# A two-stack transformer on one core: set-up constants in another queue, another order in the hybrid mixers, and mixer B's probabilities transposed head by head

## What is computed

```python
def hybrid_mixer(h, w_in, ...):
    q, k, v, z, xbc, dt = split(h @ w_in)
    attn = dilated_attention(rotary(q), rotary(k), v)          # 8 heads
    xs, bm, cm = split(silu(causal_depthwise_conv(xbc)))
    dt = softplus(dt + dt_bias)
    m = (cm @ bm.T) * segsum_exp(dt * a_neg)                   # exp(cs[l] - cs[s]) for l >= s, per head, chunks of 128
    y = m @ (xs * dt) + state_part + d_skip * xs
    return concat(attn, rmsnorm(y * silu(z))) @ w_out
# mixer B: 16 heads, compressed-block attention plus a selected-block and a window branch
o = g0 * softmax(q @ kc) @ vc + g1 * softmax(q @ k1) @ v1 + g2 * softmax(q @ k2) @ v2
```

## Time and profile before

| | us |
|---|---|
| median of 3 runs | 2666.72 (2665.9 to 2670.82) |
| the profiled execution, its own time | 2666.94 |
| span from its first to its last instruction | 2664.7 |
| PE busy | 2594.8 (97%) |
| DVE, ACT, POOL busy | 1808.8, 1449.8, 189.1 |
| mean granted TensorE clock | 0.994 of full |

### The profile page before, as it was taken

How to read it: one execution, slowest core, us unless ns; L and a number is a source line. 1 busy time by engine, 2 the same in 40 slices (tenths; PEclk the granted TensorE clock), 3 DMA queues, 4 the chain that set the end, 5 groups by cost and what they waited for, 6 DMA issues and landing times.

```text
span 2664.7 us, 43984 instructions
## 1 busy us (share of the span) xinstructions
PE 2594.8 (97%) x15457; PEld 2259.9 (85%) x15457; DVE 1808.8 (68%) x2578; ACT 1449.8 (54%) x2304; POOL 189.1 (7%) x266
## 2 busy tenths in 40 slices
PE   7999999999999999999989999999999999999999
PEld 7888888888888878888888688888888888888887
DVE  6866668666766676676676666676656667666766
ACT  4655546455555565555555655555556555555654
POOL 2010001000000030000001200000010000002000
PEclk9999999999999999999999999999999999999999
DMA  6559845487566447656654266566446666653664
GB/s 188 160 171 236 226 152 159 143 238 210 170 194 189 137 148 219 190 177 195 190 175 134 88 200 190 178 196 189 151 138 194 189 205 181 199 164 129 184 191 144
DMA packets 587098, 473.78 MB, mean 178 GB/s; under 512 B 19676, under 2 KB 546416, under 8 KB 586480
## 3 DMA queue, kind: packets, MB, share of 16 engines
q1 hardware_dynamic: 582768, 457.37, 56.6%
q0 software_dynamic: 3312, 14.36, 2.4%
q10 hardware_dynamic: 912, 0.63, 0.1%
HBM read 469.09 MB, written 6.37 MB: 178 GB/s over the span
## 4 chain that ended last, share of the span: by engine, by line
PE 86%; DVE 5%; ACT 3%; DMA 2%; issue 2%; POOL 1%; DVEq 1%; SPq 0%; POOLq 0%; ACTq 0%
PE acc L784 20%; PE gu L751 14%; PE tp L751 14%; PE tp L758 7%; PE gu L758 7%; PE acc L817 3%; DVE lo_a L454 2%; ACT hi_a L442 1%; DMA raw_a<-in_w_in 1%; PE acc L1463 1%; PE gu L1421 1%; PE gu L1430 1%; PE acc L1465 1%; PE acc L1464 1%; PE gu L1422 1%
## 5 line engine op out<-in xcount | busy, mean ns | idle before, releaser
L454 DVE TENSOR_TENSOR lo_a<-raw_a,hi_a 128x2048 fp32r<-128x2048 f32 (+1 forms) x313 | 711.1, 2272 | 359.1 <-ACT hi_a L442 357.7
L442 ACT ACTIVATE hi_a<-raw_a 128x2048 fp32r<-128x2048 f32 (+1 forms) x313 | 591.5, 1890 | 125.2 <-PE acc L1465 31.7
L751 PE MATMUL tp<-xT,hi_a 128*128 128x512 f32 x1600 | 398.4, 391 | 0.0
L751 PE MATMUL gu<-xT,hi_a 128*128 128x512 f32 x1600 | 397.9, 391 | 0.0
L751 PEld LDWEIGHTS gu<-xT,hi_a 128*128 128x128 f32 x1600 | 294.0, 188 | 56.9
L751 PEld LDWEIGHTS tp<-xT,hi_a 128*128 128x128 f32 x1600 | 293.4, 188 | 56.4
L784 PE MATMUL acc<-hi_b,h_hi 128*128 128x512 f32 x760 | 298.6, 393 | 1.3 <-issue 1.2
L784 PE MATMUL acc<-lo_b,h_hi 128*128 128x512 f32 x760 | 297.9, 392 | 0.0
L784 PE MATMUL acc<-hi_b,h_lo 128*128 128x512 f32 x760 | 295.7, 389 | 0.0
L466 DVE TENSOR_TENSOR lo_b<-raw_b,hi_b 128x1024 fp32r<-128x1024 f32 x210 | 255.9, 1219 | 0.0
L843 ACT ACTIVATE arena<-arena 128x256 f32<-128x256 f32 x200 | 83.6, 418 | 279.0 <-DVE arena L906 279.0
(11 more groups left out here) (344 smaller groups left out, 4100.8 us busy)
## 6 DMA issues: line engine op xcount, KB each, us to landing
raw_a<-in_ffn_w_in SPq DMA_DIRECT2D x352, 512.0 KB, 5.8
raw_b<-in_ffn_w_out SPq DMA_DIRECT2D x176, 512.0 KB, 3.7
raw_a<-in_w_in SPq DMA_DIRECT2D x52, 512.0 KB, 4.7
raw_a<-in_w_gate SPq DMA_DIRECT2D x44, 512.0 KB, 5.6
raw_a<-in_w_up SPq DMA_DIRECT2D x44, 512.0 KB, 6.8
raw_b<-in_w_down SPq DMA_DIRECT2D x44, 512.0 KB, 4.7
raw_a<-in_w_out SPq DMA_DIRECT2D x24, 512.0 KB, 4.3
raw_a<-in_c_w_in SPq DMA_DIRECT2D x24, 512.0 KB, 4.4
```

What stands on the lines that cost most here:

```text
L442: nc.scalar.activation(a_view(hi_a, par)[:, :, 0:width], a_view(raw_a, par)[:, :, 0:width], ACT.Copy).then_inc(a_hi, 1)
L454: nc.vector.tensor_tensor(a_view(lo_a, par)[:, :, 0:width], a_view(raw_a, par)[:, :, 0:width], a_view(hi_a, par)[:, :, 0:width].bitcast(F3 ...
L751: nc.tensor.matmul(banks[:, e, :], w_hi[:, kt, e * P:(e + 1) * P], xT[:, :, kt, :], start=(kt == 0), stop=False)
```

## The change

Four pieces. (1) **Set-up**: POOL no longer issues the nine `rest_loads`; SyncE issues them, and the seven `late_loads`, behind slot 1 and ahead of slot 2. (2) **The head of the hybrids**: `rows_pe` moves from the end of slot 0 to the middle of slot 1, between its high and low parts, with `columns_pe` behind it in the first hybrid; DVE makes the low part of slot 1 ahead of the diagonal; POOL loads the masks only after `rb_ready`. (3) **Further on in the hybrids**: at p = 11 DVE evacuates the values ahead of the low part, at p = 18 the low part of slot 10 moves ahead of the convolution (it stood behind it, at p = 19), and the addition of chunk 1's columns goes from ACT (16 exponentials with a bias) to one POOL instruction over 2048 columns (`segments_pool`); ACT then takes all four exponentials with 1024 columns each behind the high part of slot 10. (4) **Mixer B**: a unit's six blocks are transposed in two goes of three, one for each head, both into bank 0 of `tp`, 384 columns each; ACT copies each out, and the second go waits for the first copy (`head_out`). Bank 1 holds values alone. In odd steps head 0 is transposed in `middle_pe` and head 1 in `end_pe`; in even steps the values take the middle, and both heads come at the end. The waits on `o_lo` move from the transpositions to the values.

```diff
+            if s.kind == "hybrid":
+                ahead_a(lo_slot_a, dve, s.a0 + 1)
             diag_dve(dve, s)
-            ahead_a(lo_slot_a, dve, s.a0 + 1)
+            if s.kind != "hybrid":
+                ahead_a(lo_slot_a, dve, s.a0 + 1)
...
-                if s.k == 0 and i == 1:
+                if s.k == 0 and i == 2:
+                    for dst, src in rest_loads():
+                        sp.dma_start(dst, src).then_inc(rest_loaded, 16)
                     for dst, src in late_loads():
...
-                rows_pe(pe, s)
+                if s.kind != "hybrid":
+                    rows_pe(pe, s)
                 return
...
                 if low:
+                    if i == 1 and s.kind == "hybrid":
+                        rows_pe(pe, s)
+                        if s.k == 0:
+                            columns_pe(pe)
                     pe.wait_ge(a_lo, n + 1)
...
+        def segments_pool(pool, s):
+
+            pool.wait_ge(cs_out, s.layer + 1)
+            pool.wait_ge(row_in[1], 16 * (s.layer + 1))
+            nc.gpsimd.tensor_tensor(mTs[1], mTs[1], ncs[:, 16:32].unsqueeze(2).broadcast_to([P, SSM_HEADS, P]), ALU.add)\
+                .then_inc(seg_ready1, 1)
...
         def masks_pool(pool, s):
 
+            pool.wait_ge(rb_ready, s.pre + 1)
...
+        def turn_head_pe(pe, s, w, hh):
+
+            g = s.unit0 + w
+            if hh:
+                pe.wait_ge(head_out, w + 1)
+            else:
+                pe.wait_ge(prob_ready, g + 1)
+                pe.wait_ge(pt_act, g)
+                pe.wait_ge(cmp_pt_out, 2)
+            for k in range(3):
+                mm = nc.tensor.transpose(tp[:, 0, k * P:(k + 1) * P], probs[g % 3][:, hh, k * P:(k + 1) * P], ident)
+            mm.then_inc(pt_whole if hh else head_turned, 1)
+
+        def turned_head_act(act, s, w, hh):
+
+            g = s.unit0 + w
+            if hh:
+                act.wait_ge(pt_whole, g + 1)
+            else:
+                act.wait_ge(head_turned, w + 1)
+            nc.scalar.activation(probT[:, g % 2, hh * 384:(hh + 1) * 384], tp[:, 0, 0:384], ACT.Copy)\
+                .then_inc(pt_act if hh else head_out, 1)
...
             pe.wait_ge(pt_act, g + 1)
+            if s.kind == "B" and w >= 3:
+                pe.wait_ge(o_lo, s.pair0 + w // 2)
...
+            if s.kind == "B":
+                if scored(s, p - 3) is not None and scored(s, p - 3) % 2:
+                    woven_values_pe(pe, s, scored(s, p - 3))
+                elif scored(s, p - 2) is not None:
+                    turn_head_pe(pe, s, scored(s, p - 2), 0)
...
             if s.kind == "B":
-                if scored(s, p - 3) is not None and scored(s, p - 3) % 2:
-                    woven_values_pe(pe, s, scored(s, p - 3))
                 compress_pe(pe, s, p)
+                if scored(s, p - 2) is not None:
+                    if scored(s, p - 3) is not None and scored(s, p - 3) % 2:
+                        turn_head_pe(pe, s, scored(s, p - 2), 0)
+                    turn_head_pe(pe, s, scored(s, p - 2), 1)
...
             for p in b_steps():
                 i = p // 2
-                if scored(s, p - 4) is not None and scored(s, p - 4) % 2:
-                    values_act(act, s, scored(s, p - 4) // 2)
-                if scored(s, p - 3) is not None and p % 2 == 0:
-                    turned_act(act, s, scored(s, p - 3))
+                if scored(s, p - 3) is not None:
+                    turned_head_act(act, s, scored(s, p - 3), 1)
...
                     exp_act(act, s, scored(s, p - 1))
-                if scored(s, p - 3) is not None and p % 2:
-                    if p > 29:
-                        act.wait_ge(o_lo, s.pair0 + (p - 31) // 2 + 1)
-                    turned_act(act, s, scored(s, p - 3))
+                if scored(s, p - 3) is not None and scored(s, p - 3) % 2:
+                    values_act(act, s, scored(s, p - 3) // 2)
+                if scored(s, p - 2) is not None:
+                    turned_head_act(act, s, scored(s, p - 2), 0)
...
                     if p == 11:
                         rden_dve(dve, s, scored(s, p - 1))
-                    if h == 1:
+                        values_dve(dve, s, scored(s, p - 3))
+                    if p == 18 or (h == 1 and p != 19):
                         ahead_a(lo_slot_a, dve, s.a0 + i + 1)
...
-            pool.wait_ge(a_full[0], 32)
-            for dst, src in rest_loads():
-                pool.dma_start(dst, src).then_inc(rest_loaded, 16)
```

More of the change, by code:

```diff
@@ L351, in build_block @@
         score_taken = sem("score_taken")
+        seg_ready1 = sem("seg_ready1")
+        head_turned, head_out = sem("head_turned"), sem("head_out")
         score_ready, soft_ready, exp_ready, rden_ready, prob_ready = sem("score_ready"), sem("soft_ready"), sem("exp_ready"), sem("rden_ready"), sem("prob_ready")
@@ L1309, in woven_turn_pe @@
                 pe.wait_ge(pt_act, g)
-            if s.kind == "B":
-                pe.wait_ge(cmp_pt_out, 2)
-                if w >= 3:
-                    pe.wait_ge(o_lo, s.pair0 + (w - 1) // 2)
-            elif w >= 1:
+            if w >= 1:
                 pe.wait_ge(o_lo, s.pair0 + w)
@@ L1335, in woven_values_pe @@
                         cols_t = slice(512 + hh * P, 512 + (hh + 1) * P) if t else slice(hh * 256, (hh + 1) * 256)
+                        if s.kind == "B":
+                            cols_t = slice(hh * 384 + 256, (hh + 1) * 384) if t else slice(hh * 384, hh * 384 + 256)
                         mm = nc.tensor.matmul(tp[r, 1, 256 + t * P:512], v[:, t, c:c + HD], probs_t[:, cols_t],
@@ L1351, in middle_pe @@
                 ssm_middle_pe(pe, s, p)
+            if s.kind == "B":
+                if scored(s, p - 3) is not None and scored(s, p - 3) % 2:
+                    woven_values_pe(pe, s, scored(s, p - 3))
+                elif scored(s, p - 2) is not None:
+                    turn_head_pe(pe, s, scored(s, p - 2), 0)
         def end_pe(pe, s, p):
-            if scored(s, p - 2) is not None:
+            if scored(s, p - 2) is not None and s.kind != "B":
                 woven_turn_pe(pe, s, scored(s, p - 2))
@@ L1929, in hybrid_pe @@
             for i in range(14):
-                if s.k == 0 and i == 1:
-                    columns_pe(pe)
                 if i < 2:
@@ L2085, in hybrid_act @@
                         nc.scalar.activation(dec0, csd, ACT.Exp).then_inc(decays, 1)
-                    if p == 17:
-                        decay_act(act, s)
                     if p == 18:
                         ahead_a(hi_slot_a, act, s.a0 + i + 1)
-                        act.wait_ge(seg_ready, L + 1)
-                        for g in range(SSM_GROUPS):
-                            m = mTs[0][:, 8 * g:8 * g + 8, :]
-                            nc.scalar.activation(m, m, ACT.Exp).then_inc(seg_exp, 1)
+                        for c in (1, 0):
+                            act.wait_ge((seg_ready, seg_ready1)[c], L + 1)
+                            for g in range(SSM_GROUPS):
+                                m = mTs[c][:, 8 * g:8 * g + 8, :]
+                                nc.scalar.activation(m, m, ACT.Exp).then_inc(seg_exp, 1)
                     if p == 19:
@@ L2133, in silu_act @@
             nc.scalar.activation(conv[:, 2 * r:2 * r + 2, :], conv[:, 2 * r:2 * r + 2, :], ACT.Silu).then_inc(silued, 1)
-        def decay_act(act, s):
-            act.wait_ge(row_in[1], 16 * (s.layer + 1))
-            for g in range(SSM_GROUPS):
-                for h in range(8 * g, 8 * g + 8):
-                    m = mTs[1][:, h, :]
-                    ins = nc.scalar.activation(m, m, ACT.Exp, bias=ncs[:, 16 + h:17 + h])
-                ins.then_inc(seg_exp, 1)
         def square_y_act(act, s, c):
@@ L2189, in hybrid_dve @@
                         rden_dve(dve, s, scored(s, p - 1))
-                    if scored(s, p - 3) is not None:
+                    if scored(s, p - 3) is not None and p != 11:
                         values_dve(dve, s, scored(s, p - 3))
@@ L2570, in _ @@
                 if s.kind == "hybrid":
+                    segments_pool(pool, s)
                     for c in range(NT):
```

## The result

| us | before | after |
|---|---|---|
| median of 7 runs each, same chip | 2669.71 (2665.9 to 2672.07) | 2676.31 (2675.34 to 2678.85) |
| the profiled execution, its own time and span | 2666.94, 2664.7 | 2676.31, 2674.2 |
| first hybrid | 167.92 | 169.10 |
| second hybrid | 159.93 | 163.62 |
| mixer B | 169.69 | 174.67 |

The changed kernel takes 1.0031 times as long, interval 1.0022 to 1.004: slower by 6.6 us in the medians. The stage lengths run from a stage's first transposition of x (L546 after) to that of the next. The other thirteen stages agree within 0.1 us. The three differences add up to 9.85 us, some 3 more than the medians': the execution profiled before lay 2.8 us under its median, the one after on it.

A forecast was written before the change was run, and what follows sets the result against it. PE, busy for 2594.8 of 2664.7 us, bounds the kernel. +0.2 (set-up, first head), 0, 0, +0.6 (POOL) and +4.8 (mixer B) make +5.6 on 2666.94, less 0.2 for the median: 2672.3 us, range 2663 to 2678.

The forecast's parts named there:

- Mixer B: All of mixer B's stage: new waits between the two heads' transpositions and for probabilities, +4.8 us, range +2 to +7.
- The hand-over: Mixer B, even steps: PE waits uncovered for ACT's copy between the heads, 0.6 us each, +2.4 over steps 34 to 40.
- the wait for scores in step 36: Mixer B: step 36 finds ACT late, as a slot's high part stands ahead of an exponential at step 34, +0.3 us.
- the one for POOL in step 37: Mixer B: step 37 asks for probabilities 1.9 us sooner, while DVE's low part sits ahead of their reciprocal, +0.7 us.
- steps 30 to 33: Mixer B, forecast as steps 30 to 32: values come ahead of both heads at step 30, +1.2 us, between 0 and 1.7.
- rival (b): Nearly nothing: POOL lets DVE through, no half clock in the first hybrid, B at +2.5; 2665.8 us, chance 0.36 with mixtures.
- The head of the first hybrid: The wait moves from `rb` to the rotation, with half clock perhaps behind it; +0.2 us, between -1.7 and +2.
- The head of the second hybrid: The gap of 1.82 us goes but `rb` comes later, at 376.1, its chain ending at 381.3; taken as 0.
- The POOL instruction: Second hybrid: POOL's addition takes 3.6 us and delays DVE's convolution; net +0.6 us after 1.7 us of half clock goes.
- the lock: Second hybrid: POOL's addition shuts out DVE's convolution, passed down the chain to slot 11 and PE, +2.3 us.
- Slots 10 and 11, DVE's order: Hybrids: the 2.61 us gap at slot 10's low part ends, but PE waits at slot 11's instead; worth 0.
- Rival (a): The hybrids' waits really go, 12.3 us won, with B's 4.8 lost: 2659.2 us, chance 0.14.

The follow-up runs named there:

- e1: The kernel before with mixer B's part of the change alone: 2674.41 us, ratio 1.0017, mixer B 175.27 us.
- e6: e3 with the row and the gains' columns back at slot 0's end and DVE's old head order, set-up loads still on SyncE: 2659.99 us, 0.9963.
- e3: e2 without POOL's wait for the row `rb` ahead of the masks: 2666.91 us, ratio 0.9987, second hybrid 158.14 us.
- e2: The kernel before with the set-up's and hybrids' parts of the change, mixer B as before: 2671.79 us, ratio 1.0009, second hybrid 163.54 us.
- e8: The kernel before with only DVE's order in the hybrids changed (p = 11 and p = 18): 2669.51 us, ratio 0.9998.
- e5: e3 with row and DVE's head order back, columns still in slot 1, and chunk 1's addition back on ACT: 2668.33 us, against 2666.15 with it on POOL.
- e12: e6 with POOL's wait for `rb` ahead of the masks put back and the addition of chunk 1's columns on ACT: 2661.9 us, ratio 0.9971.
- e10: The kernel before with only POOL's wait for `rb` ahead of the two mask loads added: 2666.53 us, ratio 0.999, second hybrid 157.94 us.
- e9: e1 with head 0 transposed between the values in even steps and ahead of the last 3 of 12 output products in odd ones: 2673.5 us, 1.0014.

## Why the prediction was right, and where its steps were not

**The total** is right for the larger part by its reasons and for a part by compensation. Forecast were +5.6 us, measured 6.6 in the medians. The absolute number, 2672.3, lies 4.0 under the measured 2676.31 mostly because the three runs known then had a median 3.0 us under that of all seven.

**Mixer B** (+4.8): e1 measures +4.5, between 2.1 and 6.9 by its interval. The hand-over is 0.58 us where I took 0.6, ACT's copy 0.487 us (0.48 forecast), and it stands in each even step. Steps 34 to 41 grew by 3.1 us from the scores of step 34 to those of step 41 (34.22 against 31.14), against the 3.4 of these terms; the wait for scores in step 36 is 0.44 us (0.3) and the one for POOL in step 37 0.36 (0.7), with 0.35 more in step 39. For steps 30 to 33 I took +1.2, and the waits do grow by 1.2 us (2.3 to 3.5); but the half clock behind the old wait is gone, and the steps take only 0.3 us more. Up to step 30 B takes 0.9 us more, for which the sum has no term, and from step 41's scores to the end 0.7 (+0.2 forecast). So the mechanism is right and the closeness of the total is partly luck. Of rival (b)'s three terms, B at +2.5 has these waits against it, and half clock stands in the first hybrid; only what it gave for POOL is right in amount, and not by its reason.

**The head of the first hybrid**: the wait moved to the rotation, as forecast; 4.98 us (5.6) long, at 34.85 (34.2), and half clock stands behind it. The stage grew by 1.2 us, within the bounds of that term (-1.7 to +2) but also within the chance of this stage (1.8 us). What the term overlooks is that the loads' move by itself frees the row at 19.66 us (e6).

**The head of the second hybrid** is the step that failed. I took 0 and carried it to the rotation (381.3 forecast, 381.76 measured in a stage that starts 0.9 us later), and stopped there. That POOL's masks wait for `rb` has no term in the sum. Its price: two transfers of slot 4 twice as slow, 2.89 us of PE's waiting and half clock behind it; undone alone it gives back 4.9 us (e3 against e2).

**The POOL instruction** (+2.3 for the lock, net +0.6): duration (3.61 us, forecast 3.6) and exclusion are as taken. The half clock of 449 to 453.5 us did go, but came back behind slot 11's wait (0.62 over 458.5 to 463), so the 1.7 us set against the lock were not won by this. The half clock of 412 to 419 us, which the sum does not speak of, went too; e8 shows that with DVE's order. The rule of the Trainium skill (SBUF — State Buffer, "Who interferes with whom") that the one which issues first keeps the port, is borne out here with POOL first: one DVE instruction of 0.47 us lay 3.6 us beside it, in both hybrids. But "passed down the chain to slot 11 and so to PE" is wrong: the chain had slack at slot 9's high part, whose transfer landed at 440.3. And the cost of ACT's 16 exponentials, put at nothing, is about 2 us in the medians (2.2 in e5, 1.9 in e12), so that the exchange with POOL is a gain, not a loss of 0.6. In the order of before it was nothing: there the 2.61 us for slot 10's low part hid it. These errors lie against the missing masks, which is why the hybrids' sum (+0.8 forecast, +1.9 in e2) looks near.

**Slots 10 and 11, DVE's order**: worth 0, as forecast, shown alone by e8. **Rival (a)**, that the hybrids' waits really go, was not in the change as written. With the masks and the row where they do no harm it is so in the first hybrid (PE's idle time 9.4 us in e6, 15.7 before) and not in the second (9.9 and 8.7), which is shorter by the clock (0.99 and 0.97); e6 as a whole lies 9.8 us under before.

## What to carry to other kernels

When a change has several pieces, price each by itself: here the set-up loads' new place was a gain that the later place of the row and the columns took back. When a step is moved to a later place, follow everything that waits for it, on the DMA queues too: 2 MB of masks behind a row cost more than the row's own move won. A wait that a change adds can be a gain or a loss by the place of what it waits for, so try such pairs apart. And where one long chain on VectorE ends a wait, look for what lets that chain start; moving TensorE's work around it only moves the wait.

## What the runs showed of the hardware that I had not expected

- GpSimd's issue of a 1 MB transfer (1.2 us) holds a VectorE result up: two instructions of 128x128 with a float32 output took 1.18 us beside it and 0.48 us without (before against e10). VectorE itself went on: its next instruction starts at 370.49 us and takes 2.29 us in both.
- After it has issued nine small loads GpSimd stood for 6.30 us between two tiny instructions, without them 0.16 us (before against e6).
- 2 MB from GpSimd's queue in flight doubled the time of SyncE's 512 KB transfers, 11.0 us against 5.5.
- The same float32 products of TensorE in another order cost 0.25 us in 8.56 without a wait (e9 against before), and over the whole of mixer B 2 to 3 us at equal granted clock. Why stays open.
